# Key norms off a diagonal, decay rows through DRAM, and the mask on GpSimd

## The reference, cut to what matters

```python
qkv = causal_conv_silu(p[..., :GDN_QKV], conv_w)       # p = x @ w_in, 8 heads, dk 128, dv 256
q, k = l2norm(q), l2norm(k)                            # t * rsqrt(sum(t*t, -1) + 1e-6)
gc = jnp.cumsum(g, axis=-1)                            # in chunks
decay = where(causal, exp(where(causal, gc[..., :, None] - gc[..., None, :], 0)), 0)
A = where(strict, einsum('bhncd,bhnsd->bhncs', k * beta, k) * decay, 0)
uw = triangular_solve(A + eye, concat([v * beta, k * beta * exp(gc)]))   # inverse of A + I
qk = einsum('bhncd,bhnsd->bhncs', q, k) * decay
```

## Time and profile before

| | |
|---|---|
| time, median of 3 | 1157.72 us (1156.73 to 1158.68) |
| the profiled execution | 1157.23 us, of which the span 1155.4 us |
| PE busy | 1138.1 us, 98% |
| PE's weight loads | 935.1 us, 81% |
| DVE, ACT, POOL busy | 553.7 us, 504.3 us, 442.9 us |
| DMA moved | 127.74 MB, mean 111 GB/s |

### The profile page before, as it was taken

How to read it: one execution, slowest core, us unless ns; L and a number is a source line. 1 busy time by engine, 2 the same in 40 slices (tenths; PEclk the granted TensorE clock), 3 DMA queues, 4 the chain that set the end, 5 groups by cost and what they waited for, 6 DMA issues and landing times.

```text
span 1155.4 us, 17617 instructions
## 1 busy us (share of the span) xinstructions
PE 1138.1 (98%) x7072; PEld 935.1 (81%) x7072; DVE 553.7 (48%) x899; ACT 504.3 (44%) x679; POOL 442.9 (38%) x336
## 2 busy tenths in 40 slices
PE   9899999999999999999999999999999999999997
PEld 7668888888888888888788878888888888888886
DVE  2573654334451234565986655422200344676835
ACT  4474544544421124674442336755321353534532
POOL 0105555445445461433333311033544535464420
PEclk9999999999999999999999999999999999999999
DMA  9994232332332332314224211113143322323201
GB/s 347 384 385 141 88 109 73 109 109 73 109 129 74 109 112 109 109 56 110 91 61 123 73 37 37 74 41 105 73 157 109 110 78 73 111 74 111 73 1 73
DMA packets 104312, 127.74 MB, mean 111 GB/s; under 512 B 13251, under 2 KB 90801, under 8 KB 104117
## 3 DMA queue, kind: packets, MB, share of 16 engines
q1 hardware_dynamic: 99138, 119.62, 31.2%
q10 hardware_dynamic: 5107, 7.16, 1.8%
HBM read 121.53 MB, written 5.24 MB: 110 GB/s over the span
## 4 chain that ended last, share of the span: by engine, by line
PE 93%; DVE 3%; ACT 2%; DMA 1%; SPq 1%; issue 0%; POOL 0%; DVEq 0%; ACTq 0%; POOLq 0%
PE ps L273 25%; PE ps L275 25%; PE ps L274 25%; PE ps L1726 3%; PE ps L2196 1%; PE ps L2197 1%; PE ps L1732 1%; PE ps L2264 1%; PE ps L2254 1%; PE ps L2202 1%; PE ps L1752 1%; DMA pool_w<-in_pool_w 1%; PE ps L1795 1%; DMA ada<-in_ada_w 1%; PE ps L2003 1%; PE ps L2381 1%
## 5 line engine op out<-in xcount | busy, mean ns | idle before, releaser
L407 POOL TENSOR_TENSOR wl<-raw,wh 128x512 fp32r<-128x512 f32 x312 | 421.7, 1383 | 632.3 <-ACT wh L444 632.2
L273 PE MATMUL ps<-xth,wh 128*128 128x512 f32 (+1 forms) x832 | 325.6, 391 | 0.8 <-DVE xtl L1137 0.6
L275 PE MATMUL ps<-xth,wl 128*128 128x512 f32 (+1 forms) x832 | 317.6, 382 | 0.0
L274 PE MATMUL ps<-xtl,wh 128*128 128x512 f32 (+1 forms) x832 | 317.2, 381 | 0.0
L444 ACT ACTIVATE wh<-raw 128x2048 fp32r<-128x2048 f32 x78 | 149.2, 1913 | 298.9 <-PE ps L275 279.1
L273 PEld LDWEIGHTS ps<-xth,wh 128*128 128x128 f32 x832 | 156.5, 188 | 34.5 <-issue 4.8
L275 PEld LDWEIGHTS ps<-xth,wl 128*128 128x128 f32 x832 | 156.4, 188 | 30.8
L274 PEld LDWEIGHTS ps<-xtl,wh 128*128 128x128 f32 x832 | 156.7, 188 | 28.3 <-issue 0.5
L1145 DVE SCALAR_TENSOR_TENSOR conv_out<-ps,conv_taps,conv_out 128x511 f32<-128x511 f32 x44 | 32.8, 745 | 122.6 <-ACT conv_out L609 122.6
L1240 DVE SCALAR_TENSOR_TENSOR conv_v<-ps,gdn_taps,conv_v 128x511 f32<-128x511 f32 (+2 forms) x96 | 71.8, 748 | 32.6 <-ACT conv_v L677 30.0
L273 PE MATMUL ps<-wh,xth 128*128 128x512 f32 x176 | 69.7, 396 | 0.1
(11 more groups left out here) (338 smaller groups left out, 1658.3 us busy)
## 6 DMA issues: line engine op xcount, KB each, us to landing
ada<-in_ada_w SPq DMA_DIRECT2D x24, 1024.0 KB, 10.9
raw<-in_gdn_w_in SPq DMA_DIRECT2D x24, 1024.0 KB, 5.3
raw<-in_ffn_w_up SPq DMA_DIRECT2D x22, 1024.0 KB, 4.9
raw<-in_gla_w_in SPq DMA_DIRECT2D x12, 1024.0 KB, 5.1
raw<-in_ffn_w_down SPq DMA_DIRECT2D x11, 1024.0 KB, 4.9
raw<-in_gdn_w_out SPq DMA_DIRECT2D x8, 1024.0 KB, 5.0
raw<-in_gla_w_out SPq DMA_DIRECT2D x4, 1024.0 KB, 5.0
xres<-in_x SPq DMA_DIRECT2D x4, 512.0 KB, 5.0
```

Of the source, the lines that this page charges most:

```text
L273: nc.tensor.matmul(o, lh, rh, start=first, stop=False)
L274: nc.tensor.matmul(o, lh, rl, start=False, stop=False)
L275: return nc.tensor.matmul(o, ll, rh, start=False, stop=last)
L407: rest = nc.gpsimd.tensor_tensor(lo[:, part], raw[:, s, part], hi[:, part].bitcast(f32), ALU.subtract)
```

## The change

Four things change, all between units 1 and 5 of the mixer (464 to 544 us of the span).

The norms of keys: `key_diagonal(c)` on DVE multiplies the products of keys with keys by `ident` and accumulates along the row, so that `square(0)` to `square(3)`, `sums(0)`, `sums(1)` and `turn_sums(0)`, `turn_sums(1)` go, and `keys_keys()` moves to earlier chunks.

The decay rows: `gc_row()` and `dec()` go. One more matmul in `gate_sums` gives the 32 rows of decay numbers; ACT copies them (`gc_turned`), sends them to DRAM (`gc_rows`, 16 KB), and reads each half back spread over all partitions (two transfers that write 128x2048 numbers, 1 MB, into `attn`).

The mask: POOL's `mask_rows(i)` adds `mask_add` to a 128x1024 tile, two ahead of low() of unit 3 and two ahead of that of unit 4. The difference goes into exp's bias, so that `decay(i)` is eight instructions of 128x128.

The order: silu(1, 1) stands behind two decays, `root` of the first half and the negations of the second half stand later. Line numbers shift: conv_first is L699, silu L706, exp L722, high L466, low L415, key_diagonal L1285, negated L1317.

```diff
+        def keys_bank(c):
+
+            return (4, 5, 7, 6)[c % 4]
...
-            with pool.Fori(U_GIN // 2 + 2, END_GOUT // 2) as i:
+
+            def mask_rows(i):
+
+                pool.wait_ge(gc_read[i // 2], 16)
+                nc.gpsimd.tensor_tensor(attn[:, i], attn[:, i], mask_add[:].unsqueeze(1).broadcast_to([P, H, P]), ALU.add)\
+                    .then_inc(S("rows_masked"), 1)
+
+            pool.wait_ge(S("gates_ready"), 1)
+            mask_rows(0)
+            mask_rows(1)
+            low(U_GIN + 3, 0, wh[:, 1, :], wl[:, 1, :])
+            mask_rows(2)
+            mask_rows(3)
+            low(U_GIN + 4, 1, wh[:, 0, :], wl[:, 0, :])
+            with pool.Fori(U_GIN // 2 + 3, END_GOUT // 2) as i:
...
-                act.wait_ge(S("dec_diff"), 2 * i + 2)
-                nc.scalar.activation(attn[:, i], attn[:, i], ACT.Exp).then_inc(S("dec_exp"), 1)
+                act.wait_ge(S("rows_masked"), i + 1)
+                for h in range(H):
+                    dd = nc.scalar.activation(attn[:, i, h, :], attn[:, i, h, :], ACT.Exp, bias=scal[:, QA, i, h:h + 1])
+                dd.then_inc(S("dec_exp"), 1)
...
+            act.wait_ge(S("gc_mm"), 1)
+            nc.scalar.activation(gc_turned[0:TT * H, :], ps[0:TT * H, 7, 128:256], ACT.Copy).then_inc(S("gc_turned"), 1)
+            act.wait_ge(S("gc_turned"), 1)
+            act.dma_start(gc_rows, gc_turned[0:TT * H, :]).then_inc(S("gc_written"), 16)
             conv_first(0, 1)
             high_gin(2)
+            act.wait_ge(S("gc_written"), 16)
+            for half in range(2):
+                q = slice(half * TT * H // 2, (half + 1) * TT * H // 2)
+                act.dma_start(attn[:, 2 * half:2 * half + 2].rearrange("p t h c -> p (t h c)"),
+                              gc_rows[q, :].rearrange("q c -> (q c)").partition_broadcast(P)).then_inc(gc_read[half], 16)
             silu(0, 1)
-            square(0)
...
-            second(1)
-            square(1)
-            first(2)
-            sums_copy(0)
+            conv_first(1, 1)
+            high_gin(3)
             decay(0)
             decay(1)
+            silu(1, 1)
+            first(2)
             second(2)
-            square(2)
-            root(scal[:, RKI, :, 0:4])
             first(3)
             decay(2)
             decay(3)
+            root(scal[:, RKI, :, 0:4])
             second(3)
-            square(3)
             first(4)
-            sums_copy(1)
-            root(scal[:, RKI, :, 4:8])
...
-            def dec(c):
-
-                i, g = c // 2, c % 2
-                v.wait_ge(S("gcrow_mm"), c + 1)
+            def key_diagonal(c):
+
+                i, g = cell(c)
+                v.wait_ge(S("kk_mm"), c + 1)
                 for h in range(4 * g, 4 * g + 4):
-                    dd = V.scalar_tensor_tensor(attn[:, i, h, :], ps[:, cell_bank(c), (h % 4) * P:(h % 4 + 1) * P], scal[:, GC, i, h:h + 1],
-                                                mask_add[:], ALU.subtract, ALU.min)
-                dd.then_inc(S("dec_diff"), 1)
+                    dd = V.scalar_tensor_tensor(junk_d[:, h % 4], ps[:, keys_bank(c), (h % 4) * P:(h % 4 + 1) * P], 1.0, ident[:],
+                                                ALU.mult, ALU.mult, accum_out=scal[:, RKI, i, h:h + 1])
+                step(dd)
...
-            dec(0)
-            dec(1)
             taps(1, 1)
-            dec(2)
-            dec(3)
             taps(2, 0)
-            dec(4)
-            dec(5)
+            key_diagonal(0)
             taps(2, 1)
+            key_diagonal(1)
+            key_diagonal(2)
+            taps(3, 0)
+            key_diagonal(3)
             key_sums(0)
-            dec(6)
-            dec(7)
+            taps(3, 1)
             v.wait_ge(S("gc_exp"), 3)
             v.wait_ge(S("gates_ready"), 2)
             key_factors(0)
-            taps(3, 0)
             negated(0)
             negated(1)
-            taps(3, 1)
+            taps(4, 0)
             negated(2)
             negated(3)
-            taps(4, 0)
+            taps(4, 1)
+            key_diagonal(4)
+            key_diagonal(5)
+            taps(5, 0)
+            key_diagonal(6)
+            key_diagonal(7)
             key_sums(1)
+            taps(5, 1)
             key_factors(1)
-            negated(4)
-            taps(4, 1)
-            negated(5)
-            negated(6)
-            taps(5, 0)
-            negated(7)
-            taps(5, 1)
+            for c in range(4, 8):
+                negated(c)
...
-            def gc_row(c):
-
-                i, g = c // 2, c % 2
-                if c == 2:
+            def keys_keys(c):
+
+                i, g = cell(c)
+                if c == 0:
                     pe.wait_ge(S("gc_exp"), 3)
-                if c >= 3:
-                    pe.wait_ge(S("dec_diff"), c - 2)
-                for h in range(4 * g, 4 * g + 4):
-                    mm = X.matmul(ps[:, cell_bank(c), (h % 4) * P:(h % 4 + 1) * P], scal[:, GLOG, i, h:h + 1].broadcast_to([P, P]), tri[:],
-                                  start=True, stop=True)
-                mm.then_inc(S("gcrow_mm"), 1)
-
-            def keys_keys(c):
-
-                i, g = cell(c)
-                if c < 3:
-                    pe.wait_ge(S("dec_diff"), c + 6)
-                else:
-                    pe.wait_ge(S("neg_done"), c - 2)
+                elif c >= 4:
+                    pe.wait_ge(S("neg_done"), c - 3)
...
-                X.matmul(ps[:, 7, 96:128], ones[:, 0:1].broadcast_to([P, P]), glog, start=True, stop=True).then_inc(S("gc_mm"), 1)
+                X.matmul(ps[:, 7, 96:128], ones[:, 0:1].broadcast_to([P, P]), glog, start=True, stop=True)
+                X.matmul(ps[0:TT * H, 7, 128:256], glog, tri[:], start=True, stop=True).then_inc(S("gc_mm"), 1)
 
             chunk(1, 0, (3, gate_sums))
-            chunk(1, 1, (3, do(gc_row, 0)), (6, do(gc_row, 1)))
-            chunk(2, 0, (3, do(gc_row, 2)), (6, do(gc_row, 3)))
-            chunk(2, 1, (3, do(gc_row, 4)), (4, do(sums, 0)), (6, do(gc_row, 5)), end=[do(turn_sums, 0)])
-            chunk(3, 0, (3, do(gc_row, 6)), (6, do(gc_row, 7)))
-            chunk(3, 1, (3, do(keys_keys, 0)), (6, do(keys_keys, 1)))
-            chunk(4, 0, (3, do(keys_keys, 2)), (6, do(keys_keys, 3)))
-            chunk(4, 1, (2, do(sums, 1)), (4, do(keys_keys, 4)), (6, do(turn_sums, 1)))
-            chunk(5, 0, (3, do(keys_keys, 5)), (6, do(keys_keys, 6)))
-            chunk(5, 1, (3, do(keys_keys, 7)))
+            chunk(1, 1)
+            chunk(2, 0)
+            chunk(2, 1, (6, do(keys_keys, 0)))
+            chunk(3, 0, (2, do(keys_keys, 1)), (5, do(keys_keys, 2)), end=[do(keys_keys, 3)])
+            chunk(3, 1)
+            chunk(4, 0)
+            chunk(4, 1, (3, do(keys_keys, 4)), (6, do(keys_keys, 5)))
+            chunk(5, 0, (2, do(keys_keys, 6)), (5, do(keys_keys, 7)))
+            chunk(5, 1)
```

More of the change, by code:

```diff
@@ L157, in build @@
     squares = at("squares", PH, [8, 2, T])
+    junk_d = at("junk_d", PH, [4, P])
     group_sum = at("group_sum", PH + 97 * KB + 512, [2 * H])
@@ L171, in build @@
     mask_add = at("mask_add", TMP + 12 * KB, [P])
+    gc_turned = at("gc_turned", TMP + 14 * KB + 512, [P])
     junk_o = at("junk_o", TMP + 13 * KB + 512, [DV])
@@ L201, in build @@
     x_spill = nc.dram_tensor("x_spill", (T, D), f32).ap()
+    gc_rows = nc.dram_tensor("gc_rows", (TT * H, P), f32).ap()
     diag_in = nc.dram_tensor("diag_in", (4, TT * H, 32, 32), f32).ap()
@@ L218, in build @@
         ada_full = [S(f"ada_full{s}") for s in range(ADA_SLOTS)]
+        gc_read = [S("gc_read0"), S("gc_read1")]
         def bank2(b):
@@ L763, in _ @@
                     first(n)
+                if n == 5:
+                    root(scal[:, RKI, :, 4:8])
                 second(n)
@@ L1379, in _ @@
             step(V.tensor_copy(scal[:, GC], th(ps[:, 7, 64:96])))
+            step(V.tensor_scalar(scal[:, QA], scal[:, GC], -1.0, None, ALU.mult))
             V.tensor_tensor(scal[:, KDS], th(ps[:, 7, 96:128]), scal[:, GC], ALU.subtract).then_inc(S("gc_ready"), 1)
@@ L2040, in chunk, with query_squares @@
                     step()
-            def sums(n):
-                last = (2, 4, 8)[n] - 1
-                pe.wait_ge(S("sq_done"), last + 1)
+            def query_squares():
+                pe.wait_ge(S("sq_done"), 4)
                 pe.wait_ge(S("prepared"), 9)
-                if n == 0:
-                    pe.wait_ge(S("glog_done"), 1)
-                else:
-                    pe.wait_ge(S("mean_done"), 1 + 2 * TT + TT + n)
-                first = (0, 2, 4)[n]
-                for u in range(first, last + 1):
-                    j = (u - first) // 2
+                pe.wait_ge(S("neg_done"), 8)
+                for u in range(4, 8):
+                    j = (u - 4) // 2
                     for sub in range(2):
@@ L2056, in sums, with turn_query_sums @@
```

(15 more changed lines are left out.)

15 lines of the change are left out of this document (5 added, 10 removed).

## The result

The changed kernel takes 1172.03 us, median of four runs (1170.90 to 1173.19), against 1157.48 (1156.73 to 1158.68) of the kernel before beside it: a ratio of 1.0127, 95% interval 1.0115 to 1.014, so 14.5 us slower. I had said 1162.4 and at most 1167.0. The direction was right, the size was not.

A forecast was written before the change was run, and what follows sets the result against it. PE, busy 1138.1 of 1155.4 us, was taken as the bound; its 10.0 us saving goes into waits, chunk(8, 0) starting 3.7 us later. With 1.7 of clock, 1157.2 + 3.7 + 1.7 = 1162.6, given as 1162.4; range 1157.5 to 1167.

The forecast's parts named there:

- the clock: PE's clock: a fall only behind the 8 us wait ahead of chunk(8, 0), costing 1.7 us (0 to 3.4).
- key_factors: DVE, behind taps(5, 1): key_factors(1) as four operations of 0.18 to 0.25 us, from 536.8 to 537.7.
- three waits: PE: 2.5 us at keys_keys(0) for silu(1, 1), 2.2 at about 512, 8 ahead of chunk(8, 0).
- PE's saving: PE, gc_row, sums and turn_sums gone, one matmul added: 10.0 us less needed (9.5 to 10.4).
- Masks, exps, first wait: POOL, ACT, PE: masks end at 484.3, exps at 486.7, silu(1, 1) at 488.6; PE waits 2.5 us (1.7 to 3.3).
- rival of late reads: Decay-row reads land at 482.6, ACT's work 3.1 us later, time 1165.7; chance 0.21, with dear masks.
- The second wait: PE in chunk(4, 1), at about 512.3: waits for silu(3, 1), then negated(0) at 514.5; 2.2 us (1 to 4).
- The last negation: DVE's tail behind taps(5, 1): ends at 541.9 instead of 535.70, 6.2 us later (2.5 to 9).
- From there to the split of unit 8: Last negation to split of unit 8: 8.0 us of DMA plus 13.3, ending at 563.2.
- Sum: Whole kernel: 1157.2 + 3.7 (later start of chunk(8, 0)) + 1.7 (clock) = 1162.6, given as 1162.4.
- faster: Tail: last negation by 534.2, split of unit 8 by 556, up to 3.5 us gained, 1153.7; chance 0.07.

The follow-up runs named there:

- planned_order: Changed computation reordered against the changed kernel so each value comes before PE wants it, e.g. key_factors(0) ahead of taps(3, 1): 1148.16 us, 0.9924 to before.
- tail_early: Changed kernel with key_diagonal(6), (7), key_sums(1), root ahead of taps(5, 0), and key_factors(1) and four negations ahead of taps(5, 1): 1163.13 us.
- all_three: Changed kernel with the moves of silu_first, decays_later and tail_early together: 1153.68 us, 0.9962 to the kernel before.
- silu_first: Changed kernel with one move on ACT, silu(1, 1) ahead of decay(0) and decay(1) again: 1169.11 us, 1.0103 to the kernel before.
- split_in_16: Changed kernel with low() of units 5 and 7 on POOL in 16 instructions of 128 columns instead of 4 of 512: 1164.77 us, a single run.
- decays_later: Changed kernel with ACT's decay(2) and decay(3) moved behind root, second(3) and conv_first(4, 0): 1164.57 us, 1.0053 to the kernel before.
- decoupled: Changed kernel with unit 8 asked for ahead of the diagonal blocks, and taps(6, 0), taps(6, 1) ahead of the wait for diag: 1164.78 us, 1.0061 to before.
- fill_waits: Changed kernel with needless matmuls in PE's three waits: 10 ahead of keys_keys(0), 20 ahead of keys_keys(4), 46 ahead of chunk(8, 0): 1166.42 us.

## Why the prediction was right in direction and wrong in size

Two terms of the sum failed, and they make up 10.0 of the 10.4 us by which it fell short (15.8 instead of 5.4, see the sum below): the clock, which was put at nothing behind the first two waits (5.0 us more in all three), and key_factors, priced at 0.9 us where each took 3.4 (5.0 us more in both). The mechanism, three waits that the written order makes, was right.

**PE's saving** (10.0 us): right. In planned_order PE is busy 9.6 us less, and the span is 9.0 shorter.

**Masks, exps, first wait**: right within 0.2 us. The masks ended at 484.1 (484.3), the exps at 486.6 (486.7), silu(1, 1) at 488.5 (488.6), the wait was 2.6 (2.5). The reads were issued at 469.3 to 469.6 and landed within 6.3 us, by 475.9, 2 us earlier than said, which changes nothing behind the memset. The rival of late reads didn't occur; GpSimd's masks ran without a stop behind the memset.

**The clock**: this step failed first. The text took the clock for full behind the short waits ("0, as after all the short waits") and set a fall behind the third alone. That was carried over from other cases: in the kernel before the only wait above 1.4 us is the one of 2.5 with which the program starts, ahead of any matmul. The wait of 2.6 was followed by the half clock, which cost 1.6 us, and the one of 5.1 by 2.3. The third fall cost 2.8 instead of 1.7.

**key_factors**: "four of 0.18 to 0.25" was read from a place where POOL stood still. In the changed kernel both lie under a split, and each took some 3.4 us instead of 0.9: 2.5 us late twice. The evidence was in rows that I had and put aside as odd: the product of 1.23 us is of the same kind (two inputs from the on-chip memory that POOL uses too). The page that bears on it is "GPSIMD Engine Reference" of the Trainium skill (1. Specifications), which states that GpSimd shares its memory interfaces with VectorE and contends with instructions of two such inputs. The traces agree for those, and give the size: the instruction lasts until POOL's ends. Those of the same engine with one input in PSUM (the negations, the taps) kept their times under POOL's splits.

**The second wait**, 5.1 instead of 2.2: the 2.5 us of key_factors(0) account for it. The first fall of the clock made PE come later (at 513.9 instead of 512.3), and what it waits for as well, by about as much.

**The last negation**, 549.98 instead of 541.9. Of the 8.1 us, 2.9 are the longer second wait, 3.9 the two falls, 2.5 key_factors(1), and -1.1 key_diagonal at 0.21 instead of 0.35.

**From there to the split of unit 8**, 22.4 us instead of 21.3. The way of the blocks through DRAM took 9.7 instead of 8.0: its four transfers landed in 3.7 us where before it was 2.7. In tail_early and all_three it was 8.1 again, in silu_first, split_in_16, decays_later and decoupled 9.1 to 9.9, and in fill_waits, which has the order of the changed kernel, 7.9. So the written order of DVE and SP doesn't set it; why it differs is open. I also named the link wrongly: taps(6, 0) stands behind the wait for `diag`, followed by silu(6, 0), conv_first(6, 1) and high(); the text said taps(6, 1) and conv_first(7, 1). The sum was read from the trace and is not touched by it; ACT's lines under decoupled show the link.

**Sum**: chunk(8, 0) starts 13.0 us later instead of 3.7, that is 8.1 + 1.7 less the 0.5 by which the rest was shorter; with 1.1 more of clock, 5.4 becomes 15.8. (The prediction's own terms add up to 1162.6; the 1162.4 that it gives is no rounding of that.)

**The rivals**: "faster" named the right condition, negations done by the time that chunk(5, 0) ends, and put it out of reach. It was out of reach only in the order as written: planned_order, with the negations ahead of taps(5, 0), is faster by 9 us.

## What to carry to other kernels

Work taken off the busiest engine is gained only if each value that it waits for comes earlier by as much. Follow each such value through the written order of the other engines, and add the half clock behind each wait of TensorE: from 2.5 us up it came in 16 of 18 cases here, at some 2 us each. Price a small operation of VectorE with two inputs on chip outside PSUM by where it will lie: beside a long GpSimd instruction it costs what is left of that instruction.

## What the runs showed of the hardware

- Between 464 and 600 us, after a wait of PE of 3.4 us or more the clock was at 0.50 in all eleven cases (3.4 to 11.5 us, in eight kernels), and after one of 2.5 to 3.0 us in five of seven: behind 2.6 and 3.0 us in split_in_16 it stayed at 1.00. Behind 0.7 and 0.8 us it stayed too. It was low until 3.0 to 5.9 us after PE's return, at a cost of 1.5 to 2.9 us (longest in silu_first, behind the wait of 5.0).
- A VectorE operation of 16 columns with both inputs on chip outside PSUM lasted until the GpSimd instruction beside it ended: 1.2 us with pieces of 1.25 us, 0.38 with pieces of 0.42, 0.18 with none. In planned_order one took 1.34 us up to the end of POOL's split, and the next two 0.17 each. A tensor_scalar of one input was also long there (0.84 instead of 0.17 us in all_three, ending at 525.55, POOL's split at 525.52); RECIPROCAL (0.24) was not.
- Accumulating operations of 128x128 from PSUM start 0.21 us apart in a row, negations of the same size 0.26; the reading of the accumulator (83 ns) lies beside the next operation.
